# Transposes of a pair of heads in two blocks on six banks, and the work around them in a new order

## The reference

```python
o = _dense_causal(q_full, k_full, v, scale).reshape(B, S, MLA_WIDTH)
return (o * jax.nn.silu(gate)) @ w_out
```

```python
s = jnp.einsum('bqhd,bkhd->bhqk', q_blk, k) * scale
s = jnp.where(k_pos[None, :] <= q_pos[:, None], s, NEG_INF)
p = jax.nn.softmax(s, axis=-1)
return jnp.einsum('bhqk,bkhd->bqhd', p, v)
```

## Time and profile before

| what | us |
|---|---|
| median of three runs | 1680.94 |
| lowest, highest | 1676.09, 1681.35 |
| the profiled execution | 1679.65 |
| its span, first to last instruction | 1677.7 |
| PE busy in it | 1633.6 (97%) |
| DVE, ACT, POOL busy | 778.4, 769.4, 658.2 |

### The profile page before, as it was taken

One profiled execution on the slowest core, in us unless ns is written; L12 is line 12 of the kernel. 1 busy time (PEld: TensorE's weight loads), 2 busy tenths in 40 slices (PEclk: granted clock), 3 DMA queues, 4 the chain that ended last, 5 costly groups with the idle time before them and its releaser, 6 DMA issues.

```text
span 1677.7 us, 24632 instructions
## 1 busy us (share of the span) xinstructions
PE 1633.6 (97%) x9349; PEld 1337.2 (80%) x9349; DVE 778.4 (46%) x2048; ACT 769.4 (46%) x1565; POOL 658.2 (39%) x551
## 2 busy tenths in 40 slices
PE   8999999999999999999999999999999999999998
PEld 8777778887888777888777788777788888888877
DVE  3777636566353434445767636887141111001052
ACT  4565634566244535524656634337753222222252
POOL 5432134332243424225422234792154444444423
PEclk9999999999999999999999999999999999999999
DMA  6323144333542313154322145432153333333322
GB/s 172 70 48 82 39 151 143 78 68 70 155 134 76 89 52 95 51 170 105 72 55 56 51 151 169 104 101 64 61 154 101 101 100 91 98 101 88 125 63 88
DMA packets 216049, 161.19 MB, mean 96 GB/s; under 512 B 53756, under 2 KB 197148, under 8 KB 215933
## 3 DMA queue, kind: packets, MB, share of 16 engines
q1 hardware_dynamic: 205904, 130.21, 27.8%
q10 hardware_dynamic: 9804, 29.38, 5.8%
q0 software_dynamic: 224, 0.03, 0.1%
HBM read 148.32 MB, written 11.14 MB: 95 GB/s over the span
## 4 chain that ended last, share of the span: by engine, by line
PE 81%; DVE 9%; ACT 6%; issue 2%; POOL 1%; DMA 1%; ACTq 0%; DVEq 0%; SPq 0%; POOLq 0%
PE banks L543 40%; PE banks L494 8%; PE banks L496 7%; PE banks L495 7%; PE banks L776 5%; PE banks L791 4%; PE banks L735 4%; PE banks L625 4%; ACT AB L1551 2%; ACT w_hi L1421 1%; DVE banks L2409 1%; PE banks L758 1%; DVE banks L2398 1%; DVE AB L2411 1%; PE banks L964 1%
## 5 line engine op out<-in xcount | busy, mean ns | idle before, releaser
L2917 POOL TENSOR_TENSOR w_lo<-w_raw,w_hi 128x512 fp32r<-128x512 f32 (+2 forms) x506 | 617.5, 1248 | 990.1 <-ACT w_hi L1421 978.9
L1421 ACT ACTIVATE w_hi<-w_raw 128x1024 fp32r<-128x1024 f32 (+4 forms) x254 | 249.6, 994 | 161.4 <-PE banks L496 102.6
L543 PE MATMUL banks<-XTh,w_hi 128*128 128x512 f32 (+5 forms) x1216 | 292.0, 376 | 3.8 <-DVE XTl L2371 1.4
L543 PE MATMUL banks<-XTl,w_hi 128*128 128x512 f32 (+5 forms) x1216 | 279.6, 368 | 0.0
L543 PE MATMUL banks<-XTh,w_lo 128*128 128x512 f32 (+5 forms) x1216 | 271.4, 365 | 0.0
L543 PEld LDWEIGHTS banks<-XTh,w_lo 128*128 128x128 f32 (+2 forms) x1216 | 211.4, 188 | 38.0
L543 PEld LDWEIGHTS banks<-XTh,w_hi 128*128 128x128 f32 (+2 forms) x1216 | 204.9, 189 | 43.7 <-issue 8.0
L543 PEld LDWEIGHTS banks<-XTl,w_hi 128*128 128x128 f32 (+2 forms) x1216 | 208.5, 187 | 35.5
L494 PE MATMUL banks<-w_hi,OTh 128*128 128x512 f32 (+1 forms) x448 | 172.7, 386 | 0.1
L1577 ACT ACTIVATE AB<-banks 128x512 f32<-128x512 f32 (+1 forms) x200 | 101.8, 529 | 148.1 <-PE banks L776 145.1
L496 PE MATMUL banks<-w_hi,OTl 128*128 128x512 f32 (+1 forms) x448 | 167.9, 375 | 0.0
(11 more groups left out here) (230 smaller groups left out, 2211.3 us busy)
## 6 DMA issues: line engine op xcount, KB each, us to landing
w_raw<-in_w_gate_up_dram SPq DMA_DIRECT2D x44, 512.0 KB, 3.8
w_raw<-in_fox_w_in_dram SPq DMA_DIRECT2D x30, 512.0 KB, 4.1
w_raw<-in_mla_w_in_dram SPq DMA_DIRECT2D x26, 512.0 KB, 4.8
w_raw<-in_w_in_dram SPq DMA_DIRECT2D x24, 512.0 KB, 3.9
w_raw<-in_w_down_dram SPq DMA_DIRECT2D x22, 512.0 KB, 3.5
w_raw<-in_swa_w_in_dram SPq DMA_DIRECT2D x20, 512.0 KB, 4.8
w_raw<-in_mla_w_out_dram SPq DMA_DIRECT2D x16, 512.0 KB, 3.8
x_spill<-AB ACTq DMA_DIRECT2D x16, 512.0 KB, 2.7
```

The costliest lines, as they stand in the source:

```text
L543: mm = nc.tensor.matmul(o, wt[:, k, :], xt[:, k, lo:hi], start=first and n == 0 and k == 0, stop=last and n == 2 and k == nk - 1, skip_gro ...
L1421: nc.scalar.activation(view(w_hi, u, RING), view(w_raw, u, RAW), ACT.Copy).then_inc(hi_done, 1)
L2917: ins = pool.tensor_tensor(low[at], raw[at], high[at].bitcast(F32), ALU.subtract)
```

## The change

It moves instructions on three engines and adds no work of theirs; SP's and POOL's queues stay as they were. For all `late` rounds but the last of a layer:

- TensorE: the pair's transposes stand in two blocks, one for each head (10 transposes, in the window layer 7). The first stands at the round's start, the second right behind the first projection tile of the round. The six chunks have six banks. They wait for no copy, but for the maxima of pair i + 1 that read the bank last: chunk 0 for banks 4 and 5, chunk 1 for 0 and 1, chunk 2 for 2 and 3 (window layer: nothing for 4 and 5, chunk 0 for 0 and 1).
- VectorE: all chunks of `maxima(i + 2)` stand at the end of round i, ahead of `mixed(i)`. Before, chunk 0 stood there and the others behind `mixed(i)`, at the next round's start. `gated_low` stands behind `fill(i, 4)`; MLA's odd rounds have the second `norm` ahead of the maxima and no longer behind `mixed`; `low_rope` stands in the round after.
- ScalarE: the first head's exponentials of pair i + 1 stand ahead of the six copies of pair i's transposes. In MLA's odd rounds the query's high part stands right behind `gated_high`. In the forget layer the six transfers of `aug_rows` stand behind the exponentials, at position 2, where before they stood behind the mix at position 3.

```diff
+                self.t_banks = [(4, None), (5, None), (0, 0), (1, 0)] if self.window else [(4, 0), (5, 0), (0, 1), (1, 1), (2, 2), (3, 2)]
...
+            behind_tile = []
+            def tile_ended():
+                if behind_tile:
+                    behind_tile.pop()()
...
                 end(mm)
+                tile_ended()
                 weave()
...
-                    if c.tch >= 2:
+                    block = at_end and i < n_pairs - 1
+                    n = len(pr.t_chunks) * x + ch
+                    if block:
+                        read = pr.t_banks[n][1]
+                        if read is not None:
+                            pe.wait_ge(ps_free, s_first + s_len * (i + 1) + read + 1)
+                    elif c.tch >= 2:
                         pe.wait_ge(pt_free, c.tch - 1)
-                    if shared and x == 0 and ch < 2 and i + 1 < n_pairs:
-                        pe.wait_ge(ps_free, s_first + s_len * (i + 1) + 1)
...
-                        next_turn()
-                        next_turn()
-                        woven.append(next_turn)
+                        def turn_head(x):
+                            for ch in range(len(pairs[0].t_chunks)):
+                                turn(i, x, ch)
+                        turn_head(0)
+                        behind_tile.append(lambda: turn_head(1))
...
                     fill(i, 0)
+                    if pairs[0].late:
+                        exps(i + 1, 0)
                     turned(i)
                     gated_high(i - 1)
-                    if i not in exps_first:
+                    fill(i, 7)
+                    if not pairs[0].late and i not in exps_first:
                         exps(i + 1, 0)
...
-                        if pos == 5:
-                            rope(g)
-                            query(i + 3)
+                        if pos == 7:
+                            c.g += 1
+                            hi(QKh[:, 3 + (i + 3) % 2, :], group()[:, :])
+                        elif pos == 5:
+                            advance(2)
...
                 elif pos == 2 and i < 7:
+                    if i in (0, 2):
+                        act.wait_ge(ps_done, fox_s0 + 3 * (i + 2))
+                        aug_rows(i // 2 + 2)
                     advance()
                     gate(i + 1)
...
-                    elif i >= 0:
-                        for ch in range(1, s_len):
-                            maxima(i + 1, ch)
+                    fill(i, 4)
                     gated_low(i - 1)
-                    fill(i, 4)
                     norm(i + 1, 0)
...
                     elif i > -2:
-                        maxima(i + 2, 0)
+                        for ch in range(s_len):
+                            maxima(i + 2, ch)
                     if i < 0:
                         fill(i, 3)
                     mixed(i)
...
-                        elif pos == 6:
-                            low_rope(g, 1)
+                    elif pos == 4 and i < 5:
+                        low_rope((i + 2) // 2, 0)
+                    elif pos == 6 and i < 5:
+                        low_rope((i + 2) // 2, 1)
...
-                pair_attention(mla_pairs(), fill, norm_last=(1, 3))
+                pair_attention(mla_pairs(), fill)
```

More of the change, by code:

```diff
@@ L412, in s_bank, with t_bank @@
                 return bank[(self.s_banks[ch] if self.late else 2 * (n % 2)) + x]
+            def t_bank(self, n, block):
+                return bank[self.t_banks[n][0] if block else 4 + n % 2]
             def score(self, b, x, t):
@@ L704, in pair_attention @@
                 at_end = pairs[0].late
-                shared = at_end and not pairs[0].window
                 def scores(i, ch):
@@ L722, in scores @@
                         pe.wait_ge(ps_free, c.sch - s_len + 1)
-                    if shared and ch == 0 and c.tch:
+                    if at_end and ch == 0 and c.tch:
                         pe.wait_ge(pt_free, c.tch)
@@ L775, in turn @@
                             col = pr.at[t] + j * P - ((t + 1) * P - pr.keys[t])
-                            mm = nc.tensor.transpose(bank[4 + c.tch % 2][:, o:o + P], SBP[a % 2][x][:, col:col + P], ident[:, :])
+                            mm = nc.tensor.transpose(pr.t_bank(n, block)[:, o:o + P], SBP[a % 2][x][:, col:col + P], ident[:, :])
                             o += P
@@ L824, in pair_attention @@
                         todo = []
-                        rest = [(x, ch) for x in range(2) for ch in range(len(pairs[0].t_chunks))]
-                        def next_turn():
-                            if rest:
-                                turn(i, *rest.pop(0))
-                        next_turn()
-                        next_turn()
-                        woven.append(next_turn)
+                        def turn_head(x):
[3 more added lines that the diff above has]
+                        behind_tile.append(lambda: turn_head(1))
                     if i == n_pairs - 1:
@@ L855, in pair_attention @@
                     if at_end and i < n_pairs - 1:
-                        woven.pop()
-                        while rest:
-                            next_turn()
+                        assert not behind_tile
                         if i > -2:
@@ L1573, in turned @@
                     for x in range(2):
-                        for js in pr.t_chunks:
+                        for ch, js in enumerate(pr.t_chunks):
                             act.wait_ge(pt_done, c.tch + 1)
                             width = pr.t_width(js)
+                            src = pr.t_bank(len(pr.t_chunks) * x + ch, pr.late and i < n_pairs - 1)
                             nc.scalar.activation(PTP[x][:, pr.pt[js[0]]:pr.pt[js[0]] + width],
-                                                 bank[4 + c.tch % 2][:, 0:width], ACT.Copy).then_inc(pt_free, 1)
+                                                 src[:, 0:width], ACT.Copy).then_inc(pt_free, 1)
                             c.tch += 1
@@ L1974, in fill @@
                             values(half, FOX_VALUES[i] % 2)
-                    if i in (0, 2):
-                        act.wait_ge(ps_done, fox_s0 + 3 * (i + 2))
-                        aug_rows(i // 2 + 2)
             fox_s0 = 8 * (3 + 2)
@@ L2569, in fill @@
                             query(i + 3)
-                            if i > 0:
-                                keys(g, 0)
                             rope_sum()
@@ L2576, in fill @@
                                 gate_at[2] = c.g
+                            keys(g, 0)
                         elif pos == 2:
-                            if i < 0:
-                                keys(g, 0)
                             keys(g, 1)
```

4 lines of the change are left out of this document (3 added, 1 removed).

## The result

The changed kernel takes 1707.92 us (median of four runs, 1705.11 to 1709.24), the kernel before 1680.36 beside it. The ratio is 1.0166, 95% interval 1.0149 to 1.0182: slower by 27.6 us. The forecast was slower, 1691 us; the time lies above its range of 1676 to 1700.

A forecast was written before the change was run, and what follows sets the result against it. TensorE was taken as the bound, busy 1633.6 of 1677.7 us. New waits summed to 1679.65 + 9.0 (two MLA layers) + 1.8 (window layer) + 0.5 (forget layer) = 1690.95, forecast as 1691 us, range 1676 to 1700.

The forecast's parts named there:

- The even round's step: MLA even rounds: late copies delay chunk 0's maxima, so the next round's first transposes wait +0.7 us, +0.3 after round 0.
- The odd round's step: MLA odd rounds: waits of 1.25 us to the second key tile, 3.35 to 3.95 in all against 2.81; took +0.55.
- The second value half: MLA odd rounds: it waits for the gated mix's bank, 2.1 us, or up to 2.7 if the second head's exponentials hold.
- The rope's wait: MLA odd rounds: TensorE's key-tile stall for the rope's product, 1.67 us before, was to be no wait any more.
- Rival 1's point of decision: Faster outcome, 1659 or 1668 us, chance 0.13: holds if even rounds' chunk 0 is read before 15.63, not at 16.3.
- The granted clock is 1.00 in both: TensorE's clock read as full in an even and an odd round of MLA layer 0; no cost for it in the sum.
- 275 ns for a transpose: The skill's price, 2.75 us for ten in a block; the prediction said the trace's 0.106 us each contradicted it.
- the lower end: MLA odd rounds: +0.55 us taken from a range of +0.55 to +1.1, since the sum had no gaps of its own.
- window and forget layer: Window layer +1.8 us (0 to +3) from a late gate bank; forget layer +0.5 us (-2 to +4).
- rounds 4 to 6 of an MLA layer: End of each MLA layer: existing waits for maxima grow and the third chunk waits, +0.7, +1.2 and +0.5 us.
- `aug_rows`: Forget layer: moving its transfers removes a 2.4 us wait for a copy, less 0.5 of new waiting: -1.9 us.
- rival 3: Slower, 1699 us, chance 0.1: regular window and forget rounds also wait for maxima, 0.5 to 0.7 in each of 14.

The follow-up runs named there:

- the experiment without blocks: Changed kernel with transposes again in chunks on two banks and the first head's exponentials again behind the copies, the rest of the change kept: 1690.35 us.
- first value half made twice: Changed kernel with TensorE repeating the first value half in MLA's rounds 1 and 3, unneeded work that fills part of the 2.5 us wait: 1698.22 us.
- chunk 0 early: Changed kernel without blocks, VectorE reordered in MLA: chunk 0's maxima ahead of gate product (rounds 0, 2, 4, 5), mix ahead of maxima (rounds 1, 3): 1663.52 us.

## Why the prediction was wrong, step by step

**Right: the direction and the mechanism.** The even round's step gave a first block held up 0.7 by chunk 0; it is 0.88 in round 3, and 0.36 in round 1, where 0.3 stood. The odd round's step gave 1.25 up to the second key tile; it is 0.31 + 0.95 = 1.26. The second key tile starts 9.35 into the round where the sum said 9.45. The second value half waits 2.5, inside the 2.1 to 2.7 that stood there. The rope's wait is gone, and the experiment without blocks shows that the late copies are the blocks' doing. Rival 1's point of decision, the copies' end, is decided by the blocks: with them off, the even rounds do not wait.

**Wrong: a term that was not in the sum, the clock.** "The granted clock is 1.00 in both" was read from rounds whose longest stall is 1.67 us, and then carried over to a kernel for which the same text forecast stalls of 2.1 to 2.7. The trace of before had a sign outside the rows that I read, though a mixed one. It has three waits of 2.0 us or more in the late layers; behind those in the first MLA layer (2.0) and in the forget layer (2.4) the clock stays, but at round 6 of the second MLA layer TensorE waits 2.0 us for maxima, and the stretches there are

```profile
944.00:948.00 4.00, 2.16 (x16) 0.86 (x12) 3.37 (x15) 0.49 (x2) 0.45 (x1) 1.00 0.44 131
948.00:952.00 4.00, 3.81 (x15) 3.41 (x16) 3.49 (x17) 1.47 (x3) 0.00 (x0) 0.57 0.00 0
```

with the same 0.57 as behind the value halves. In the changed kernel the other three waits of 2.5 are followed by a fall too, and so are the waits at round 6 of both layers, 1.9 us long (below, the first, third and fourth line stand behind waits of 2.5, the second and fifth at round 6):

```profile
176.00:180.00 4.00, 4.00 (x21) 3.73 (x21) 0.00 (x0) 3.21 (x11) 0.00 (x0) 0.70 0.00 0
212.00:216.00 4.00, 3.69 (x13) 2.89 (x12) 2.69 (x11) 1.94 (x7) 0.00 (x0) 0.57 0.00 0
897.00:901.00 4.00, 2.83 (x15) 2.83 (x16) 2.45 (x7) 0.23 (x1) 0.00 (x0) 0.70 0.03 8
938.00:942.00 4.00, 3.08 (x17) 3.08 (x18) 2.23 (x5) 0.64 (x2) 0.00 (x0) 0.70 0.01 2
976.00:980.00 4.00, 3.69 (x16) 3.00 (x16) 3.21 (x15) 1.42 (x6) 0.00 (x0) 0.64 0.00 0
```

One fall costs about 1.55 us (first value half made twice). Five more falls than before make 7.8 of the 11.1 us by which TensorE's busy time grew. About 3 more come with the blocks and not with the clock: the two kernels without a fall in the late layers have 1630.4 us (chunk 0 early) and, with blocks, 1633.5. By which matmuls, I did not separate. The Trainium skill ("TensorE: Matmul & The Clock Gate", "Why this matters for your kernels") warns of idle gaps between bursts of matmuls; the trace agrees in kind, but the falls of the changed kernel came behind waits shorter than the gap it names, and the measurement decides. By it the stalls that I forecast would have passed as harmless, so it would not have mended the sum.

**A reading that was wrong and changed nothing.** I set 275 ns for a transpose against 0.106 us in a block and called it a contradiction. One is how long a single transpose lasts, the other the pitch: in the profile of the kernel before the 672 of them last 276 ns on average, and eight of them still start 0.106 apart. And a clock of 1.00 around a block of 0.85 us between full tiles cannot test the rest of that sentence.

**Wrong: the lower end.** The odd round came out at +0.55 to +1.1 and I took 0.55, "since the sum has no gaps of its own". It has one: the gated output's low part takes 1.78 instead of the 0.61 that I used, because its new place lies beside GpSimd's split (moved away from it, it takes 0.69). By idle time alone an odd round loses 0.31 + 0.95 + 0.30 + 2.50 = 4.06 against 2.81: +1.25, beyond the upper end. The prediction asked whether GpSimd's queue was changed, which it was not; it should have asked what runs beside the moved instruction. The trace of before had a case, outside the rows that I read: in round 3 the rope's sum lasts 1.25 beside GpSimd's subtractions, 0.68 in round 1.

```profile
160.61 1.25 DVE L2530 TENSOR_TENSOR AB<-AB,G 128x512 f32<-128x512 f32 x1
```

**Mis-sized: window and forget layer.** +3.0 instead of 1.8, +2.4 instead of 0.5, both within the ends that I gave (+3, and -2 to +4), both nearer to the upper one. In the forget layer each regular round loses 0.5 to 0.9 where I had 0.35, and not at the third tile's bank: five tiles wait for a late split of a weight (3.0 us in the list, L555 behind `w_hi`; before, 0.4 once). In round 5 of every late layer the scores and in round 6 the mix wait 0.8 to 0.9 for copies (all of the 3.5 and 3.5 of the 4.1 us in the list), which I had not asked about. With them rounds 4 to 6 of an MLA layer have 3.1 us more idle time where I had 2.4, although their waits for maxima grew by only 1.0. `aug_rows` gains 1.8, as forecast (1.9).

**The range.** Its upper end was rival 3, more waits of the same sort. It had no case in which a wait costs more than its length, and the uncertain terms were all taken at or below their middle. With the odd rounds at their upper end (4 x 0.55 more) and five falls (7.8), the sum would have been 1701, 7 short instead of 17.

## What to carry to other kernels

When an edit makes the critical engine wait longer, price the wait and then look in the trace for what such a wait did to the engine's clock: here 2.5 us idle cost 4 where the clock fell behind it. When work is put into fewer, larger blocks, see who reads the first piece, because everything behind the last piece in the reader's queue moves by the block's delay, and cover it as the exponentials did here. On an engine that has idle time but stands on the path at a round's end, the order of its queue is the whole matter: with the blocks taken out, moving one chunk of maxima into an idle 1.5 us, the mix ahead of the rest, and a low part and a norm with them turned 0.6% of loss into 1.0% of gain.

## What the runs showed of the hardware

TensorE's granted clock fell to its lower level behind idle waits and was back at 1.00 within the next four to eight us; more work on TensorE in such a wait made the kernel 10 us faster. The length of a wait alone does not decide. In the twelve traces (their first 20 us left out) a fall begins in the wait, or within 2 us behind it, for 13 of 14 waits of 2.9 to 4.1 us, for 14 of 23 of 2.4 to 2.5, for 11 of 29 of 1.9 to 2.3, and for none of 89 of 1.2 to 1.8. The same code differs between executions: at round 6, behind 1.9 to 2.0 us, it fell in both MLA layers of the changed kernel, in one of two before, and in none with the first value half made twice. Nine falls stand behind no such wait; six of them are at one place behind the second MLA layer, in both kernels too, where the longest wait is 0.98. What decides there stays open.

A VectorE subtraction with both inputs in SBUF (128x512, the gated output's low part) took 0.69 us alone and 1.78 while GpSimd's subtractions ran beside it throughout: in the late layers four of 32 in the changed kernel, none of 32 before, none of 32 when it was moved out of the way. The Trainium skill ("SBUF — State Buffer", "Who interferes with whom") says that such an instruction of VectorE contends with GpSimd instructions that read SBUF; the trace agrees, and 1.1 us is its price here. Subtractions with one input in a PSUM bank took 0.69 beside GpSimd's too. So the engines meet at more than the semaphores. Not each instruction with both inputs in SBUF pays: the rope's sum of the kernel before took 0.68 in round 1, with GpSimd's subtractions beside it as well.
